# The order of an inverse and a forward transform inside two slots of a hybrid encoder kernel

## The chip, the cores and the metric

The kernel runs on one core of one Trainium2 chip. The metric is the device time of one launch in microseconds. The core has five engines with a queue each: TensorE (PE in the rows, its weight loads PEld), VectorE (DVE), ScalarE (ACT), GpSimd (POOL), and SyncE (SP), which here only starts transfers. They meet at semaphores.

## The reference, cut to what matters

One encoder layer is applied to two sequences, 512 and 256 tokens long, with 1024 features and float32 values. One large projection feeds windowed attention, an order-2 Hyena long convolution and two gates; the branches are merged and projected, and an MLP and a last norm follow. The change concerns the Hyena branch alone. Each of its two rounds convolves 512 channels with a filter as long as the sequence, by a Fourier transform, and multiplies by another row set:

```python
def long_conv(u, spec, bias):
    L = u.shape[1]
    uf = u.astype(jnp.float32)
    y = jnp.fft.irfft(jnp.fft.rfft(uf, n=2 * L, axis=1) * spec[None], n=2 * L, axis=1)[:, :L]
    return y + uf * bias.astype(jnp.float32)
...
    z = x1.astype(jnp.float32) * long_conv(v, spec[:, 0], hyena_bias[0])
    z = x2.astype(jnp.float32) * long_conv(z, spec[:, 1], hyena_bias[1])
```

## The kernel before, in words

All matmuls of the projection keep features on the partitions and the 768 tokens of both sequences along the free axis, in two halves of 384. Float32 precision comes from splitting each operand into a high and a low part and adding three products. Before the merge there are 34 **slots** (`t` from 0 to 33, `T_MERGE` = 34). In each slot TensorE runs `gemm(t)`: one 128-column weight tile against the whole input, 48 matmuls on L739. Behind the gemm it runs the **stages** that the list `STAGES[t]` names. The same list is read by the loops of ScalarE and VectorE, so one list sets the order on three engines: on TensorE and ScalarE as it stands, on VectorE sorted so that an inverse always comes last. Slots 18 to 33 compute the gate columns.

**The Hyena work** is cut into six steps (`STEPS`, numbered 0 to 5 in the code): for each of the two rounds two channel halves of the long sequence, then the whole short sequence. Steps 0, 1, 3 and 4 are the long ones (`LONG`); the "second and fifth step" are numbers 1 and 4. A step goes through this chain:

- `fold(n)`, GpSimd (L655 to L681): sums and differences of each row with its mirror image. A long step takes four instructions (L673, L674, L680, L681), a short one two (L680, L681).
- `turn(n)`, TensorE (L968, matmuls on L981): eight transposes into two PSUM banks. ScalarE copies their high part (L1403), VectorE takes the low part (L2030).
- `forward(n)`, TensorE (L984): for a long step 12 matmuls of 512 columns on L995 into four banks.
- `cosines_out(n)`, ScalarE (L1412), long steps only: copies banks 0 and 2 (L1423).
- `products(n)`, VectorE; for a long step `products_long` (L1967): four rotations (L1977, L1978), which count up `rot_done` after each pair, two multiplications by the filter spectrum over 2048 columns (L1986, L1987), two sums over 1024 columns (L1990, L1991), four `scalar_tensor_tensor` instructions that write the product tile Y (L1997, L1998). The writes of Y first wait for the previous step's inverse, which reads the same tile.
- `inverse(n)`, TensorE (L1010): 32 matmuls of 128 columns on L1029 into two banks, 16 for each.
- `inverse_out(n)`, ScalarE (L1425): copies the two banks (L1431).
- `unfold(n)`, GpSimd (L683): four instructions for a long step (L695, L696, L698, L699), two for a short one (L702, L703).
- `combine(n)`, VectorE (L2040, instruction L2047): the multiplication by the other rows.

GpSimd's own order is written out by hand: `fold(0)`, and then for each n `fold(n + 1)`, `unfold(n)`. So `fold(2)` stands behind `unfold(0)` in its queue, and `fold(5)` behind `unfold(3)`.

**PSUM banks.** The stages share four banks of the tensor `wk` in rotation. A planner (`use`, `bank_of`, `last_reader`, L307 to L339) walks the slots in the order of `STAGES`, gives each use the next bank and has `take` (L928) wait until the last reader of the bank's previous content is done. A long forward's four banks are released by its two cosine copies and its two pairs of rotations in turn.

**Other queues.** SyncE loads the weight tile of slot t + 2 and, in odd slots from 21 on, the two spectrum tiles of the step whose turn stands in slot t (L521), after the previous step's products are done. ScalarE and VectorE split the weight tile of slot t + 2 (L1249, L1691) ahead of their stages of slot t.

The stages of the slots concerned: slot 20 has forward 0, slot 21 turn 1, slot 22 inverse 0 and forward 1, slot 23 turn 2, slot 24 inverse 1 and forward 2, slot 25 turn 3 and inverse 2, slot 26 forward 3, slot 27 turn 4, slot 28 inverse 3 and forward 4, slot 29 turn 5, slot 30 inverse 4 and forward 5, slot 31 inverse 5.

Of the kernel before, what the change touches and what calls it, by code (L numbers as in the profile page):

```python
# [50 lines left out]
T_Q, T_K, T_V, T_HY, T_GATE, T_MERGE, T_OUT, T_MLP = 0, 4, 5, 6, 18, 34, 42, 50  # L51
# [13 lines left out]
LONG = [n for n, (u, _) in enumerate(STEPS) if UNITS[u][0] == 0]  # L65
# [8 lines left out]
STAGES = {t: [] for t in range(T_MERGE)}  # L74
# [3 lines left out]
for _n in range(len(STEPS)):  # L78
    STAGES[T_GATE + 1 + 2 * _n].insert(1 if _n == 0 else 0, ("turn", _n))
    if _n - 1 in LONG:  # L80
        STAGES[T_GATE + 2 + 2 * _n].append(("inverse", _n - 1))
    STAGES[T_GATE + 2 + 2 * _n].append(("forward", _n))
    if _n not in LONG:
        STAGES[T_GATE + 3 + 2 * _n].append(("inverse", _n))

# [2508 lines left out]
```

## Time and profile before

| what | value |
|---|---|
| three runs | 1138.15, 1138.93, 1141.29 us |
| median | 1138.93 us |
| the profiled execution, its time | 1140.42 us |
| its span, first to last instruction | 1138.9 us |
| TensorE busy | 1103.2 us, 97% |
| VectorE busy | 815.6 us, 72% |
| ScalarE busy | 436.4 us, 38% |
| GpSimd busy | 110.7 us, 10% |
| mean granted TensorE clock | 0.993 |

The span is what the engines' records cover; the profiled execution's own time is 1.5 us more. Starts in timelines count from the span's start. A duration in a timeline runs from the instruction's start to its end and includes what it was held up by once it had begun; the time in square brackets is idle time of the engine ahead of it, with what ended it. The granted clock is a share of TensorE's full 2.4 GHz, so that 0.50 is 1.2 GHz.

### The profile page before, as it was taken

Reading aid. Unit: us, or ns where it says so; the run is one execution under the profiler, and the core shown is the slowest. Engines: PE = TensorE matmul, PEld = TensorE weight load, DVE = VectorE, ACT = ScalarE, POOL = GpSimd, SP = SyncE. Lnnn points to the kernel's source line nnn. Section 1 sums busy time; section 2 is a strip of 40 time slices with the busy share of each in tenths; the row PEclk is TensorE's granted clock in tenths of the full one; section 3 lists DMA queues with packets and bytes.
Section 4 is the critical chain, followed back from the end, with each engine's and each line's share of the span. In section 5 each row is a group of like instructions: output and inputs, shape, how many; then the busy total and the mean of one; then the engine's idle time right before and its main releaser. Section 6 shows DMA issues by size and latency. Waiting matters only on the chain. (4 is left out here: it accounts for less than half of the span.)

```text
span 1138.9 us, 16657 instructions
## 1 busy us (share of the span) xinstructions
PE 1103.2 (97%) x6322; PEld 1026.1 (90%) x6322; DVE 815.6 (72%) x1375; ACT 436.4 (38%) x748; POOL 110.7 (10%) x132
## 2 busy tenths in 40 slices
PE   6999999999999999999999999999999999999996
PEld 4777788888899998999889999998999999999886
DVE  5878998778667677456547677687877878688534
ACT  5722145445532222422326332153352625257424
POOL 3101210000314532000000000000000000000000
PEclk9999999999999999999999999999999999999998
DMA  9925572231342332564312342133223323222203
GB/s 351 404 68 171 188 246 87 83 102 40 120 136 102 102 102 102 171 231 140 108 40 111 101 140 74 55 129 107 99 93 111 103 84 116 89 75 74 93 20 111
DMA packets 45525, 138.85 MB, mean 122 GB/s; under 512 B 5051, under 2 KB 10635, under 8 KB 44556
## 3 DMA queue, kind: packets, MB, share of 16 engines
q1 hardware_dynamic: 29024, 80.21, 21.0%
q0 software_dynamic: 11376, 44.84, 11.2%
q10 hardware_dynamic: 5052, 12.81, 3.2%
q8 instruction: 47, 0.77, 0.3%
q14 instruction: 26, 0.21, 0.0%
HBM read 121.61 MB, written 15.74 MB: 121 GB/s over the span
## 5 line engine op out<-in xcount | busy, mean ns | idle before, releaser
L739 PE MATMUL acc_ps<-act_hilo,w_hi 128*128 128x384 f32 x1536 | 339.6, 342 | 2.1 <-DVE w_lo L1691 1.2
L739 PEld LDWEIGHTS acc_ps<-act_hilo,w_hi 128*128 128x128 f32 x1536 | 270.4, 189 | 20.8 <-issue 19.4
L739 PE MATMUL acc_ps<-act_hilo,w_lo 128*128 128x384 f32 x768 | 195.9, 336 | 0.0
L739 PEld LDWEIGHTS acc_ps<-act_hilo,w_lo 128*128 128x128 f32 x768 | 139.5, 189 | 0.0
L1173 PE MATMUL acc_ps<-hidden_hilo,act_hilo 128*128 128x384 f32 x768 | 135.0, 335 | 0.6 <-DVE hidden_hilo L2240 0.4
L1173 PEld LDWEIGHTS acc_ps<-hidden_hilo,act_hilo 128*128 128x128 f32 x768 | 133.1, 188 | 1.9 <-issue 1.0
L1691 DVE TENSOR_TENSOR w_lo<-w_raw,w_hi 128x1024 fp32r<-128x1024 f32 x62 | 76.6, 1236 | 67.7 <-ACT w_hi L1249 66.4
L1249 ACT ACTIVATE w_hi<-w_raw 128x1024 fp32r<-128x1024 f32 x62 | 65.2, 1053 | 40.5 <-PE acc_ps L739 36.9
L2126 DVE SCALAR_TENSOR_TENSOR xT<-acc_ps,modT,xT 128x512 f32<-128x512 f32 (+1 forms) x32 | 19.7, 617 | 61.3 <-PE acc_ps L818 61.1
L2251 DVE SCALAR_TENSOR_TENSOR xT<-acc_ps,modT,xT 128x384 f32<-128x384 f32 (+2 forms) x96 | 40.5, 477 | 31.4 <-PE acc_ps L1173 31.4
L1782 DVE CUSTOM_DVE_ANT_0 dot_out<-dot_ring,c_rows,vecT 128x1024 f32<-128x1024 f32 x48 | 61.6, 1283 | 0.9
L739 PE MATMUL acc_ps<-hidden_hilo,w_hi 128*128 128x384 f32 x256 | 54.7, 334 | 0.0
L1473 ACT ACTIVATE gates_out<-acc_ps 128x768 f32<-128x768 f32 x16 | 13.0, 812 | 102.8 <-PE acc_ps L739 102.8
L818 PE MATMUL acc_ps<-hidden_hilo,w_down_hilo 128*128 128x512 f32 (+1 forms) x288 | 50.2, 336 | 0.0
L818 PEld LDWEIGHTS acc_ps<-hidden_hilo,w_down_hilo 128*128 128x128 f32 x288 | 44.4, 190 | 5.6
L1154 PE MATMUL wk<-act_hilo,w_hi 128*128 128x384 f32 x192 | 48.7, 334 | 0.0
L1154 PE MATMUL wk<-t_hilo,w_hi 128*128 128x384 f32 x192 | 48.7, 334 | 0.0
L2233 DVE TENSOR_TENSOR c_st<-wk,c_st 128x384 f32<-128x384 f32 x84 | 44.7, 550 | 1.7 <-PE wk L1154 1.1
L739 PEld LDWEIGHTS acc_ps<-hidden_hilo,w_hi 128*128 128x128 f32 x256 | 45.3, 188 | 0.0
L2240 DVE TENSOR_TENSOR hidden_hilo<-c_st,hidden_hilo 128x384 fp32r<-128x384 f32 x48 | 26.8, 557 | 23.6 <-ACT hidden_hilo L1585 23.3
L1566 ACT ACTIVATE act_hilo<-w_raw 128x512 fp32r<-128x512 f32 x32 | 20.0, 626 | 59.0 <-PE acc_ps L1173 59.0
L1557 ACT ACTIVATE w_hi<-s_sum 128x512 fp32r<-128x512 f32 x24 | 14.9, 627 | 64.2 <-DVE s_sum L2208 64.2
(284 smaller groups left out, 2017.2 us busy)
## 6 DMA issues: line engine op xcount, KB each, us to landing
w_raw<-in_w_pre SPq DMA_DIRECT2D x50, 512.0 KB, 3.5
dot_ring<-in_w_ada_cols POOLq DMA_DIRECT2D x48, 512.0 KB, 3.9
w_raw<-in_w_up SPq DMA_DIRECT2D x32, 512.0 KB, 3.9
w_raw<-in_w_down SPq DMA_DIRECT2D x16, 512.0 KB, 3.5
w_raw<-in_w_down_half SPq DMA_DIRECT2D x32, 256.0 KB, 2.6
spec<-filt_out POOLq DMA_DIRECT2D x12, 512.0 KB, 3.9
gate_spill<-gates_out ACTq DMA_DIRECT2D x16, 384.0 KB, 2.5
hy_spec<-spec SPq DMA_DIRECT2D x12, 512.0 KB, 5.2
```

The lines of the kernel that those rows point to most:

```text
L739: mm = pe.matmul(acc_ps[:, slot, 512 * h:512 * h + HALF], w[:, kw, :], src[:, x, k, HALF * h:HALF * h + HALF], start=(first and i == 0), s ...
L818: mm = pe.matmul(acc_ps[:, slot, half(h)], w_i[:, k, :], src[:, x, k, half(h)], start=(n == 0 and i == 0), stop=(n == KD - 1 and i == 2))
L1154: mm = pe.matmul(st_ps(q, j), w[:, k, :], st_act(j, x, k), start=(k == 0 and i == 0), stop=(k == PK - 1 and i == 2))
L1173: mm = pe.matmul(acc_ps[:, m % 2, 512 * h:512 * h + HALF], w[:, k, :], hid[:, x, k, HALF * h:HALF * h + HALF], start=(k == 0 and i == 0), ...
L1249: act_e.activation(whi[s][:] if to is None else to[0], raw[s][:], ACT.Copy).then_inc(hi_done, 1)
L1566: act_e.activation(st_weight(ST_DOWN[m % 3])[0], quarter(m % 4), ACT.Copy).then_inc(sd_hi, 1)
L1691: dve.tensor_tensor(lo, raw[s][:], hi, ALU.subtract).then_inc(lo_done, 1)
L1782: dve.tensor_tensor_reduce(junk[:], ring[:, i], cb[:, g], 1.0, vT[:, V_BA + mt:V_BA + mt + 1], ALU.mult, ALU.add, modT[:, mt, g:g + 1]).th ...
L2126: dve.scalar_tensor_tensor(row, acc_ps[:, s, half(h)], modT[:, gate + m, h:h + 1], row, ALU.mult, ALU.add)\
L2233: dve.tensor_tensor(dst, st_ps(q, j), other, ALU.add).then_inc(st_u, 1)
L2240: dve.tensor_tensor(hid_block(q, b, 1), c_block(b), hid_block(q, b, 0), ALU.subtract).then_inc(h4_lo, 1)
L2251: last = dve.scalar_tensor_tensor(xT[:, m, a:b], acc_piece(s, a, b), modT[:, G2 + m, g:g + 1], xT[:, m, a:b], ALU.mult, ALU.add)
```

## The change

In the list of stages, `forward` is no longer appended in even slots. It is inserted at the front for long steps, and at place 1 for short ones:

```diff
     STAGES[T_GATE + 1 + 2 * _n].insert(1 if _n == 0 else 0, ("turn", _n))
     if _n - 1 in LONG:
         STAGES[T_GATE + 2 + 2 * _n].append(("inverse", _n - 1))
-    STAGES[T_GATE + 2 + 2 * _n].append(("forward", _n))
+    STAGES[T_GATE + 2 + 2 * _n].insert(0 if _n in LONG else 1, ("forward", _n))
     if _n not in LONG:
         STAGES[T_GATE + 3 + 2 * _n].append(("inverse", _n))
```

The lists that differ are those of slots 22 and 28: forward 1 ahead of inverse 0, and forward 4 ahead of inverse 3. Slots 20 and 26 hold a forward alone; in slots 24 and 30 a short forward at place 1 stands behind the inverse as it did. No instruction of work is added or removed. Three things follow from the list by program: TensorE's order and ScalarE's order in the two slots, and the banks there. The inverse now takes the places of the forward's first two banks, so its first half waits for the first cosine copy and its second half for the first pair of rotations.

## Rows read from the trace of the kernel before

**Rows 1.** the profile page, part 1: busy time of each engine over the span

```profile
PE 1103.2 (97%) x6322; PEld 1026.1 (90%) x6322; DVE 815.6 (72%) x1375; ACT 436.4 (38%) x748; POOL 110.7 (10%) x132
```

**Rows 2.** the waits of TensorE: waiter <- releaser, total us, times, longest

```profile
PE wk L981 <- POOL hy_fold L681: 4.8, 2, 2.4
```

**Rows 3.** TensorE's timeline, slots 22 to 24: start, us, line, [idle before <-releaser]

```profile
334.18 3.73 PE L1029 MATMUL wk<-dft_inv,hy_prod 128*128 128x128 f32 x32
337.67 0.47 PE L995 MATMUL wk<-hy_foldT_hi,dft_fwd_hi 128*128 128x512 f32 x1
...
340.52 0.87 PE L739 MATMUL acc_ps<-act_hilo,w_hi 128*128 128x384 f32 x4
...
351.41 1.97 PE L981 MATMUL wk<-ident,hy_fold 128*128 128x128 f32 x8 [2.38 <-POOL hy_fold L681]
...
354.83 0.86 PE L739 MATMUL acc_ps<-act_hilo,w_hi 128*128 128x384 f32 x4
```

**Rows 4.** TensorE's timeline of the second stall, in slot 29

```profile
429.46 1.89 PE L981 MATMUL wk<-ident,hy_fold 128*128 128x128 f32 x8 [2.38 <-POOL hy_fold L681]
```

**Rows 5.** TensorE: the clock granted at 352 us (busy, clock, DMA, GB/s)

```profile
352.00:353.00 1.00, 1.00 (x7) 0.50 0.07 16
```

**Rows 6.** TensorE's timeline, slots 25 to 27

```profile
379.90 3.84 PE L1029 MATMUL wk<-dft_inv_p,hy_prod 128*128 128x128 f32 x32 [1.71 <-DVE hy_prod L2023]
...
391.90 0.39 PE L995 MATMUL wk<-hy_foldT_hi,dft_fwd_hi 128*128 128x512 f32 x1
...
403.01 1.04 PE L981 MATMUL wk<-ident,hy_fold 128*128 128x128 f32 x8
...
404.96 0.85 PE L739 MATMUL acc_ps<-act_hilo,w_hi 128*128 128x384 f32 x4
```

**Rows 7.** ScalarE's timeline, slot 22, then slot 26

```profile
337.95 0.60 ACT L1431 ACTIVATE hy_halves<-wk 128x512 f32<-128x512 f32 x1 [1.19 <-PE wk L1029]
...
393.76 1.08 ACT L1423 ACTIVATE hy_cosines<-wk 128x512 f32<-128x512 f32 x2
```

**Rows 8.** GpSimd's timeline, slots 22 and 23

```profile
338.63 1.29 POOL L695 TENSOR_TENSOR hy_pairs<-hy_halves 128x512 f32<-128x512 f32 x1 [29.44 <-ACT hy_halves L1431]
...
341.25 1.29 POOL L698 TENSOR_TENSOR hy_y<-hy_pairs 128x512 f32<-128x512 f32 x1
342.50 3.34 POOL L699 TENSOR_TENSOR hy_y<-hy_pairs 128x512 f32<-128x512 f32 x1
345.81 3.33 POOL L680 TENSOR_TENSOR hy_fold<-hy_xv 128x512 f32<-128x512 f32 x1
349.11 2.25 POOL L681 TENSOR_TENSOR hy_fold<-hy_xv 128x512 f32<-128x512 f32 x1
```

**Rows 9.** VectorE's timeline, slots 22 and 23

```profile
342.27 2.42 DVE L1986 TENSOR_TENSOR hy_cross<-hy_turned,hy_spec 128x2048 f32<-128x2048 f32 x1
344.62 3.38 DVE L1987 TENSOR_TENSOR hy_turned<-hy_turned,hy_spec 128x2048 f32<-128x2048 f32 x1
348.03 2.19 DVE L1990 TENSOR_TENSOR hy_turned<-hy_turned,hy_cross 128x1024 f32<-128x1024 f32 x1
350.15 2.29 DVE L1991 TENSOR_TENSOR hy_turned<-hy_turned,hy_cross 128x1024 f32<-128x1024 f32 x1
```

**Rows 10.** VectorE's timeline, slot 26

```profile
395.77 0.74 DVE L1978 SCALAR_TENSOR_TENSOR hy_turned<-hy_cosines,vecT,wk 128x512 f32<-128x512 f32 x1
...
397.96 2.29 DVE L1986 TENSOR_TENSOR hy_cross<-hy_turned,hy_spec 128x2048 f32<-128x2048 f32 x1
...
402.49 1.23 DVE L1990 TENSOR_TENSOR hy_turned<-hy_turned,hy_cross 128x1024 f32<-128x1024 f32 x1
...
404.88 0.75 DVE L1997 SCALAR_TENSOR_TENSOR hy_prod<-hy_turned,vecT 128x512 f32<-128x512 f32 x1
```

**Rows 11.** the queue that loads the spectra, and the landing times of those loads

```profile
331.16 1.20 SPq L521 DMA_DIRECT2D hy_spec<-spec  x2
...
DMA to landing us min/median/max: 4.3/5.2/7.0
```

## The prediction

> **What bounds the kernel now.** The page's first part comes first: TensorE is busy for 97% of the span [rows 1], so a microsecond counts only where TensorE loses or wins it. The waits of TensorE come next: two of them, 4.8 us together, are the transposes of a turn waiting for the last GpSimd instruction of a fold [rows 2]. The timeline puts the first in slot 23: gemm 23 has run out, TensorE is idle for 2.38 us, and turn 2 starts at 351.41 [rows 3]. The second has the same length in slot 29, ahead of turn 5 at 429.46 [rows 4]. These are exactly the slots behind the two that the change touches.
>
> Each stall has a second price. At 352 us the granted clock is 0.50, the lower level of 1.2 GHz, though TensorE is busy all the while [rows 5]. From the turn's start to the second group of high-part matmuls of the next gemm it takes 354.83 - 351.41 = 3.42 us [rows 3]; the same stretch in slot 27, where nothing was waited for, takes 404.96 - 403.01 = 1.95 us [rows 6]. So a stall now costs 2.38 us plus 1.47 us of slow clock. After the wait of 1.71 us in slot 25 an inverse takes 3.84 us against 3.73 [rows 3, 6], so a wait of that length brings no slow clock.
>
> Why is the fold late? GpSimd's timeline shows a chain of six instructions in its queue: the four of unfold 0, from 338.63, and the two of fold 2, ending at 349.11 + 2.25 = 351.36 [rows 8], 0.05 us before the turn. The first three take about 1.25 us each, the last three 3.34, 3.33 and 2.25. VectorE's timeline beside it reads like a zip: L1986 ends at about 344.62, the fourth GpSimd instruction ends 1.2 us later at 345.84; L1987, which had started at 344.62, takes 3.38 instead of some 2.2, to 348.00; the next GpSimd instruction ends at 349.14, L1990 at 350.22, the last GpSimd one at 351.36, L1991 at 352.44 [rows 8, 9]. Undisturbed, L1986 takes 2.29 and L1990 1.23 [rows 10]. So GpSimd's additions and VectorE's two-input operations on SBUF exclude each other for whole instructions, and take turns. Net durations in this zip are 1.15 us for one of GpSimd, 2.2 for a large and 1.1 for a small one of VectorE.
>
> **The change, part by part.** In slot 22 an inverse and a forward change places on TensorE and ScalarE; slot 28 repeats it with steps 3 and 4. Nothing is added or removed, so TensorE's work costs the same. The inverse takes 337.67 - 334.18 = 3.49 us and the forward 340.52 - 337.67 = 2.85 us [rows 3].
>
> *Forward 1* moves ahead by 3.49 us and starts at 334.18. Slot 26 has a forward with no inverse ahead of it and is the pattern: forward at 391.90 [rows 6], two cosine copies back to back from 393.76 [rows 7], the first pair of rotations done at 395.77 + 0.74 = 396.51, L1986 at 397.96 [rows 10]. Carried over, the first copy starts 1.86 us after the forward, at 336.04, and half of their 1.08 us later it is done, at 336.6; the first rotations are done at 334.18 + 4.61 = 338.79; L1986 starts at 334.18 + 6.06 = 340.24, some 2.2 us before it can really work today. The spectrum that L1986 reads was ordered from 331.16 in two issues, done by 332.36, and such loads land after at most 7.0 us [rows 11]: 339.4 at the latest, so this stays hidden by a margin of 0.9.
>
> *The inverse's new waits.* It starts at 334.18 + 2.85 = 337.03, after the copy that its first bank needs. Its second half starts 1.75 us later, at 338.78, when the rotations that it now waits for are just done. I take 0.1 us. Queued behind it on TensorE is gemm 23, and behind that gemm lies a stall of 2.38 us; up to this length the wait costs nothing, so the sum has 0 for it.
>
> *Unfold 0.* The second half of the inverse is copied at 337.95 now, 3.77 us after the inverse's start, in 0.60 us [rows 7], and GpSimd begins 0.08 us after that. Afterwards: 337.03 + 3.77 + 0.60 + 0.08 = 341.48, which is 2.85 us later. Queued behind it on GpSimd is fold 2, and for fold 2 waits turn 2. **This is what the change costs.**
>
> *The zip.* With both starts known I lay out the turns. L1986 holds from 340.24 to 342.44. GpSimd 1 (waiting since 341.48) to 343.6, L1987 to 345.8, GpSimd 2 to 346.95, L1990 to 348.05, GpSimd 3 to 349.2, L1991 to 350.3, GpSimd 4 to 351.45. Now VectorE comes to the four L1997 and L1998, 0.75 us each with the next starting after about 0.66 [rows 10]. Their two tensors lie in SBUF too, but no row shows such an instruction beside GpSimd. The bounds: they don't exclude GpSimd, or they do like the rest. The nearest rows are those of L1990 and L1991 [rows 9], with two SBUF inputs also, so I take the second: L1997 to 352.1, GpSimd 5 to 353.25, L1998 to 353.9, GpSimd 6 to 355.05. Turn 2 starts at 355.1 instead of 351.41: **3.7 us** later. If they don't exclude it, the last two run in 1.25 us each after 351.45, and the turn starts at 354.0, 2.6 us later.
>
> On this the Trainium skill has a rule (SBUF — State Buffer, section Who interferes with whom): a VectorE instruction with two SBUF inputs contends with a GpSimd instruction that reads SBUF, and the later one fully blocks until the other is done. The trace agrees for the plain additions and multiplications; for `scalar_tensor_tensor` no row shows it, and by the rule the turn would be late by the 3.7, not the 2.6.
>
> *The slow clock.* It is there already. The stall grows from 2.4 to about 6 us, of which no row here has an example in mid-kernel. The nearest row is the present stall, so I add nothing; bounds: it could save its 1.47 us, or cost once more as much.
>
> *Other work.* VectorE's writes of Y (from about 351.5) wait for inverse 0, done by 340.6: free. It ends combine 0 and the weight split for slot 25 near 359, while gemm 24 starts near 356.7 and, like gemm 23 (340.52 to 351.41 - 2.38), takes 8.5 us: hidden. SyncE's next spectrum load is ordered after that, against a need that itself moved by 3.7 us: hidden. Turn 2 takes the banks of the forward's third and fourth use, read long before. In slot 24 both VectorE and GpSimd start from TensorE's work again, so the shift passes on unchanged, with the 1.71 us wait of slot 25 [rows 6].
>
> **Sum.** Two slots by 3.7 is 7.4 us. From the profiled execution: span 1138.9 + 7.4 = 1146.3, and its own time 1140.42 + 7.4 = 1147.8. That execution was 1.5 us above the median of the runs, so against the median: 1138.93 + 7.4 = **1146.3 us**.
>
> **The rivals.**
> - *The four L1997 and L1998 do not exclude GpSimd.* Two slots by 2.6 is 5.2: 1144.1 us. For it speaks only that no row shows the clash. Chance 0.17.
> - *The longer stall is also a longer stretch of slow clock,* 1.47 us more in each: 1149.2 us. Against it: the clock is at its lower level already and had no further to fall. Chance 0.13.
> - *It comes out faster.* One mechanism: at the shared access to SBUF GpSimd wins every time once it has begun. Then its six instructions run from 342.44 in about 7.2 us, turn 2 starts at 349.7, 1.7 us earlier than now, and with a stall of only 0.7 us the slow clock would go too: 2 x (1.7 + 1.47) = 6.3 us, 1132.6 us. It decides when VectorE's large operations come to lie behind the GpSimd chain; what counts is a turn before 351.41. For it speaks that VectorE's operations do start 2.2 us earlier relative to TensorE; against it the strict turns of today's rows. Chance 0.04.
> - *No change to be told.* The no-clash case (5.2) together with a slow clock that by luck is over sooner (up to 2.9 saved) gives 2.3 and 1141.2 us. Chance 0.06.
>
> **How the numbers follow.** My forecast (1146.3) has 0.60, the four rivals 0.40. A measurement of this kernel can tell about 0.3%, 3.4 us, from no change. Slower by more than that: forecast, no-clash and longer slow clock, 0.90. Within: 0.06. Faster: 0.04. The range goes from the no-clash case less 0.8 of the runs' spread, 1143.3, to the longer slow clock plus the same, 1150.0; the faster and the unchanged case stay outside.
>
> **What would show it.** In the profile afterwards: TensorE's wait for L681 at 12 us in two, not 4.8; GpSimd's chain in slot 22 starting about 7.3 us after the slot's first stage with its first instruction already stretched to some 2 us; L1986 starting 2 us earlier relative to the forward's old place. From the first stage of slot 22 to turn 2 it takes 351.41 - 334.18 = 17.2 us now; I forecast 20.9, the no-clash case gives 19.8, and anything under 18.5 refutes both, or if L1998 beside a GpSimd instruction keeps its 0.75 us.

## The result and the profile after

The changed kernel takes 1148.58 us in the median of six runs (1146.21 to 1151.99), against 1139.32 us of the kernel before in the runs beside it: a ratio of 1.0081, 95% interval 1.0058 to 1.0104. It is slower by 9.3 us, with 6.6 to 11.9 us left open by the interval. The forecast was 1146.3 us, 7.4 us over the median of 1138.93 us that it started from.

The page's first part, after, answers to [rows 1]. TensorE's work is 0.7 us more, the span 8.0 us more (1138.9 to 1146.9), so most of what was lost is idle time:

```profile
PE 1103.9 (96%) x6322; PEld 1026.2 (89%) x6322; DVE 821.1 (72%) x1375; ACT 436.4 (38%) x748; POOL 111.8 (10%) x132
```

The waits of TensorE (waiter, releaser, total, times, longest) answer to [rows 2]. The first went from 4.8 to 11.1 us, 6.3 us more; the other, in slots 25 and 31, is what it was:

```profile
PE wk L981 <- POOL hy_fold L681: 11.1, 2, 5.6
...
PE wk L1029 <- DVE hy_prod L2023: 2.1, 2, 1.7
```

TensorE's timeline of slots 22 to 24, and of the second place in slots 28 to 29 (answers to [rows 3, 4]):

```profile
334.64 0.39 PE L995 MATMUL wk<-hy_foldT_hi,dft_fwd_hi 128*128 128x512 f32 x1
...
337.41 3.94 PE L1029 MATMUL wk<-dft_inv,hy_prod 128*128 128x128 f32 x32
341.11 0.94 PE L739 MATMUL acc_ps<-act_hilo,w_hi 128*128 128x384 f32 x4
...
355.26 1.97 PE L981 MATMUL wk<-ident,hy_fold 128*128 128x128 f32 x8 [5.56 <-POOL hy_fold L681]
...
358.69 0.85 PE L739 MATMUL acc_ps<-act_hilo,w_hi 128*128 128x384 f32 x4
...
416.12 0.39 PE L995 MATMUL wk<-hy_foldT_hi,dft_fwd_hi 128*128 128x512 f32 x1
...
436.74 1.97 PE L981 MATMUL wk<-ident,hy_fold 128*128 128x128 f32 x8 [5.56 <-POOL hy_fold L681]
...
440.37 0.86 PE L739 MATMUL acc_ps<-act_hilo,w_hi 128*128 128x384 f32 x4
```

The forward now begins slot 22's stages at 334.64, the inverse follows at 337.41, gemm 23 at 341.11. Turn 2 comes 355.26 - 334.64 = 20.62 us after the first stage; before it was 17.23. The stall ahead of it is 5.56 us, not 2.38. The turn and the start of the next gemm take 358.69 - 355.26 = 3.43 us, as before (3.42). In the second place the figures are 436.74 - 416.12 = 20.62 against 429.46 - 412.24 = 17.22, 5.56 against 2.38, and 440.37 - 436.74 = 3.63 against 433.05 - 429.46 = 3.59. So between the two traces 3.39 + 3.40 = 6.8 us lie in the two stretches from the slot's first stage to the turn: 3.18 us in each stall, and 0.2 us in each inverse ahead of it. Of the other 1.2 us of the spans' difference, 0.46 lies ahead of slot 22, where the kernels are the same, and 0.7 behind slot 29.

GpSimd's timeline, the same six instructions as in [rows 8]:

```profile
342.06 2.08 POOL L695 TENSOR_TENSOR hy_pairs<-hy_halves 128x512 f32<-128x512 f32 x1 [32.41 <-ACT hy_halves L1431]
344.10 3.34 POOL L696 TENSOR_TENSOR hy_pairs<-hy_halves 128x512 f32<-128x512 f32 x1
347.51 2.15 POOL L698 TENSOR_TENSOR hy_y<-hy_pairs 128x512 f32<-128x512 f32 x1
349.62 2.25 POOL L699 TENSOR_TENSOR hy_y<-hy_pairs 128x512 f32<-128x512 f32 x1
351.83 1.71 POOL L680 TENSOR_TENSOR hy_fold<-hy_xv 128x512 f32<-128x512 f32 x1
353.50 1.71 POOL L681 TENSOR_TENSOR hy_fold<-hy_xv 128x512 f32<-128x512 f32 x1
```

And VectorE's beside it, answering to [rows 9, 10]:

```profile
338.51 0.74 DVE L1978 SCALAR_TENSOR_TENSOR hy_turned<-hy_cosines,vecT,wk 128x512 f32<-128x512 f32 x1
...
340.69 2.29 DVE L1986 TENSOR_TENSOR hy_cross<-hy_turned,hy_spec 128x2048 f32<-128x2048 f32 x1
342.90 3.38 DVE L1987 TENSOR_TENSOR hy_turned<-hy_turned,hy_spec 128x2048 f32<-128x2048 f32 x1
346.32 2.19 DVE L1990 TENSOR_TENSOR hy_turned<-hy_turned,hy_cross 128x1024 f32<-128x1024 f32 x1
348.44 2.31 DVE L1991 TENSOR_TENSOR hy_turned<-hy_turned,hy_cross 128x1024 f32<-128x1024 f32 x1
350.78 1.64 DVE L1997 SCALAR_TENSOR_TENSOR hy_prod<-hy_turned,vecT 128x512 f32<-128x512 f32 x1
352.34 1.75 DVE L1998 SCALAR_TENSOR_TENSOR hy_prod<-hy_turned,vecT 128x512 f32<-128x512 f32 x1
354.01 1.74 DVE L1997 SCALAR_TENSOR_TENSOR hy_prod<-hy_turned,vecT 128x512 f32<-128x512 f32 x1
355.68 0.74 DVE L1998 SCALAR_TENSOR_TENSOR hy_prod<-hy_turned,vecT 128x512 f32<-128x512 f32 x1
```

All six of GpSimd's are stretched now, where three were before. Read the two lists as one: L1986 begins at 340.69 with nothing in its way, and the first GpSimd instruction, begun at 342.06, waits it out (2.08 us instead of 1.25). From there the ends alternate: GpSimd 344.14, VectorE 346.28, GpSimd 347.44, VectorE 348.51, and so on. The last four of VectorE are the `scalar_tensor_tensor` of which no row beside GpSimd stood ahead of the prediction: there three of them take 1.64 to 1.75 us, the fourth, alone, 0.74. They exclude GpSimd like the rest.

Measured from the slot's first stage, GpSimd's chain starts 342.06 - 334.64 = 7.42 us in, where it started 338.63 - 334.18 = 4.45 us in before [rows 8], 2.97 us later. From its first start to its last end it takes 355.21 - 342.06 = 13.15 us, where it took 351.36 - 338.63 = 12.73. So of the 3.39 us by which it ends later, 2.97 are the later start and only 0.42 are added stretching.

TensorE's granted clock in the second place (stretch, length, busy, clock, DMA share, GB/s):

```profile
432.00:433.00 1.00, 0.00 (x0) 1.00 0.11 43
...
435.00:436.00 1.00, 0.00 (x0) 0.50 0.00 0
...
438.00:439.00 1.00, 1.00 (x6) 0.50 0.00 0
...
440.00:441.00 1.00, 1.00 (x6) 0.86 0.00 0
```

The clock fell during the idle time, stood at 1.2 GHz for the rest of it and for the first 3.5 us or so of work, then rose. In the first place it fell late: by half-microseconds the granted clock is 1.00 up to 354.5 us, 0.94 up to 355.0, 0.50 from there to 358.0 and 0.65 up to 358.5, so that about 3.1 us of work lie at the low level there.

### The profile page after: what moved, and what is told of

Its sections match the earlier page's. It is cut to its first block and busy times, and to the rows that moved or that the text cites. A ratio compares the mean times of both kernels' runs of the same rounds, so it can differ in the third digit from the quotient of the medians.

```text
span 1146.9 us, 16657 instructions
## 1 busy us (share of the span) xinstructions
PE 1103.9 (96%) x6322; PEld 1026.2 (89%) x6322; DVE 821.1 (72%) x1375; ACT 436.4 (38%) x748; POOL 111.8 (10%) x132
```

## The experiments

All runs are single-core and timed in turns with the kernel before, on one chip for each group of four (the last group has two); ratios are to the kernel before in the same group, whose median lay between 1140.5 and 1141.3 us there (for the change itself it is the ratio of the section above, beside 1139.32 us). A second ruler beside the time is the distance in the trace from slot 22's first stage to turn 2, and from slot 28's to turn 5: it holds nothing of the drift from run to run.

| kernel | ratio, 95% interval | slot 22 to turn 2, us | turn 2 to the gemm's second group, us | slot 28 to turn 5, us |
|---|---|---|---|---|
| before | 1 | 17.23 | 3.42 | 17.22 |
| the change | 1.0081 [1.0058, 1.0104] | 20.62 | 3.43 | 20.62 |
| slot 22 alone | 1.0040 [1.0025, 1.0056] | 20.62 | 3.36 | 17.22 |
| slot 28 alone | 1.0032 [1.0017, 1.0048] | 17.22 | 3.45 | 20.62 |
| the change, fold first | 0.9942 [0.9922, 0.9962] | 14.88 | 1.94 | 14.90 |
| before, fold first | 0.9930 [0.9907, 0.9954] | 14.68 | 1.95 | 14.68 |
| the change, products held | 1.0002 [0.9988, 1.0017] | 15.12 | 1.97 | 15.09 |
| before, products held | 0.9997 [0.9987, 1.0007] | 14.68 | 1.94 | 14.68 |
| the change, stall filled | 1.0046 [1.0030, 1.0063] | 20.64 | 1.98 | 20.65 |
| before, stall filled | 0.9957 [0.9941, 0.9973] | 17.21 | 1.97 | 17.23 |

**One slot at a time.** The condition of the change is `_n == 1` in the one kernel and `_n == 4` in the other:

```diff
-    STAGES[T_GATE + 2 + 2 * _n].insert(0 if _n in LONG else 1, ("forward", _n))
+    STAGES[T_GATE + 2 + 2 * _n].insert(0 if _n == 1 else 1, ("forward", _n))
```

> The order is changed in slot 22 alone; slot 28 stays as before. Theory A (the late inverse holds up the fold in GpSimd's queue, the same in both slots, and each of the two is on the path by itself): half of the loss, about 4 us over before (3.4 us more stall, some tenths of slow clock), with TensorE's wait of 5.6 us in slot 23 and of 2.4 us in slot 29. Theory B (the new wait of the inverse on the rotations carries the loss): also half, but with TensorE's stall in slot 23 unchanged at 2.4 us and the time lost ahead of gemm 23. Theory C (the loss is one of the two alone): 0 or 8 us.

> The order is changed in slot 28 alone. Theory A: about 4 us over before, wait of 2.4 us in slot 23 and 5.6 us in slot 29. Theory C: the complement of the first run.

Measured: 1145.38 us and 1143.99 us, by the ratios 4.6 us (2.9 to 6.4) and 3.6 us (1.9 to 5.5) over the kernel before. TensorE's timeline, slot 22 alone:

```profile
354.13 1.97 PE L981 MATMUL wk<-ident,hy_fold 128*128 128x128 f32 x8 [5.58 <-POOL hy_fold L681]
...
432.10 1.94 PE L981 MATMUL wk<-ident,hy_fold 128*128 128x128 f32 x8 [2.37 <-POOL hy_fold L681]
```

and slot 28 alone:

```profile
351.40 1.73 PE L981 MATMUL wk<-ident,hy_fold 128*128 128x128 f32 x8 [2.37 <-POOL hy_fold L681]
...
433.05 1.97 PE L981 MATMUL wk<-ident,hy_fold 128*128 128x128 f32 x8 [5.58 <-POOL hy_fold L681]
```

The stall is 5.58 us where the order is changed and 2.37 us where it is not. The loss is two equal losses that add up. Theory C falls. Theory B falls too: it wanted the time lost ahead of gemm 23 and the stall left at 2.4 us.

**The fold ahead of the unfold.** GpSimd's order is changed and nothing else. `fold(2)` needs turn 1 and rows that nobody writes, and `fold(5)` needs turn 4 and what the combine of step 2 wrote, so they need not stand behind `unfold(0)` and `unfold(3)`:

```diff
             fold(0)
             for n in range(len(STEPS)):
-                if n + 1 < len(STEPS):
+                if n + 1 < len(STEPS) and n + 1 in LONG:
                     fold(n + 1)
+                if n + 2 < len(STEPS) and n + 2 not in LONG:
+                    fold(n + 2)
                 unfold(n)
```

> The changed kernel with one more edit on GpSimd: fold 2 stands ahead of unfold 0 and fold 5 ahead of unfold 3 in its queue. Theory A: turn 2 and turn 5 no longer wait for anything, so both stalls (2 x 5.6) and their slow clock (2 x 1.5) go: 14 us under the changed kernel, 1134 to 1135 us, under the kernel before too. Theory B: the inverse's wait stays and only the part that stood there before (2 x 3.9) goes: about 1140 us.

> The kernel before with the same edit on GpSimd. Both theories: its two stalls of 2.4 us and their slow clock go, 7.7 us, to about 1131.5 us. Theory A: within 1 us per slot of the run before this one, since the order of the two transforms then has nothing left to hold up; theory B: that run stays 7 to 8 us slower than this one.

Measured: 1134.61 us on the changed kernel, 1131.98 us on the one before. TensorE's timeline of the first (lines stand two lower in these kernels):

```profile
334.08 0.39 PE L997 MATMUL wk<-hy_foldT_hi,dft_fwd_hi 128*128 128x512 f32 x1
...
348.96 1.04 PE L983 MATMUL wk<-ident,hy_fold 128*128 128x128 f32 x8
...
449.12 3.84 PE L1031 MATMUL wk<-dft_inv_p,hy_prod 128*128 128x128 f32 x32 [1.76 <-DVE hy_prod L2025]
```

and of the second:

```profile
332.79 3.73 PE L1031 MATMUL wk<-dft_inv,hy_prod 128*128 128x128 f32 x32
...
347.47 1.04 PE L983 MATMUL wk<-ident,hy_fold 128*128 128x128 f32 x8
...
446.05 3.84 PE L1031 MATMUL wk<-dft_inv_p,hy_prod 128*128 128x128 f32 x32 [0.39 <-DVE hy_prod L2025]
```

Neither turn waits. The change that cost 3.4 us a slot costs 14.88 - 14.68 = 0.2 us a slot once the fold is out of the way. That 0.2 is the inverse's new wait on the rotations: the inverse takes 3.94 us in the trace after, against 3.73 [rows 3], and in its middle, at 339.3 to 339.6 us, there are fewer matmuls than elsewhere in it; the first pair of rotations ends at 338.51 + 0.74 = 339.25. Some 1.4 us more are in slot 31, where inverse 5 waits 1.76 us for VectorE's products instead of 0.39. Those products begin later too, 438.35 us against 435.37 in the other kernel, or 2.4 us after forward 5 against 1.2; why was not tested. In three other places of the same trace VectorE waits for a spectrum load, 3.8 us together, and nowhere in the other kernel's. The two spans differ by 3.5 us; 1.3 of it lies ahead of slot 22. So theory A holds, with a small part of B beside it. The kernel before with the fold first is the fastest kernel of this study, 0.7% under the kernel before (interval 0.5 to 0.9%).

**The clash taken away, the late start left.** In steps 1 and 4 VectorE waits with its large operations until GpSimd is through:

```diff
                 dve.wait_ge(rot_done, m + 2)
+                if n in (1, 4):
+                    dve.wait_ge(fold_done, n + 2)
                 z = Z[:].rearrange("p k (i o) n -> p k i (o n)", o=2)
```

> The changed kernel; in steps 1 and 4 VectorE waits with L1986 until GpSimd has finished the next fold. GpSimd's queue keeps its order and its late start; only the clash with VectorE is taken away. Theory A with the zip as its second half (the inverse's 2.85 us alone would be hidden): GpSimd's six instructions take 7.5 us from 342.1 and end at 349.6, when gemm 23 ends too; the stall is under 0.5 us instead of 5.6, the slow clock goes, and the time is about 14 us under the changed kernel, 1134 to 1136 us. Rival (the start of the unfold is what counts, the clash little): the stall shrinks by less than 2 us a slot. Second rival (VectorE now late, inverse 1 and forward 2 wait for it): the stall moves to slot 24 and little is won.

> The kernel before with the same wait on VectorE. Theory A: GpSimd's chain ends at 346.2, well inside gemm 23; both stalls and their slow clock go, 7.7 us: about 1131.5 us. Second rival: VectorE's products end some 4 us later than before and slot 24 waits for them.

Measured: 1140.90 us and 1139.48 us, where some 1135 and 1131.5 were expected. GpSimd's timeline of the changed kernel so held:

```profile
341.48 1.30 POOL L695 TENSOR_TENSOR hy_pairs<-hy_halves 128x512 f32<-128x512 f32 x1 [32.41 <-ACT hy_halves L1431]
342.74 1.29 POOL L696 TENSOR_TENSOR hy_pairs<-hy_halves 128x512 f32<-128x512 f32 x1
344.11 1.29 POOL L698 TENSOR_TENSOR hy_y<-hy_pairs 128x512 f32<-128x512 f32 x1
345.35 1.28 POOL L699 TENSOR_TENSOR hy_y<-hy_pairs 128x512 f32<-128x512 f32 x1
346.59 1.28 POOL L680 TENSOR_TENSOR hy_fold<-hy_xv 128x512 f32<-128x512 f32 x1
347.83 1.29 POOL L681 TENSOR_TENSOR hy_fold<-hy_xv 128x512 f32<-128x512 f32 x1
```

TensorE's:

```profile
334.06 0.39 PE L995 MATMUL wk<-hy_foldT_hi,dft_fwd_hi 128*128 128x512 f32 x1
...
349.18 1.09 PE L981 MATMUL wk<-ident,hy_fold 128*128 128x128 f32 x8
...
378.83 6.63 PE L1029 MATMUL wk<-dft_inv_p,hy_prod 128*128 128x128 f32 x32 [3.72 <-DVE hy_prod L2025]
```

Six instructions at 1.25 us, none stretched, although the first starts 7.4 us after the slot's first stage, as late as in the changed kernel. Turn 2 comes at 15.12 us, not 20.62. This is the split that was wanted: with the clash taken out of both kernels the late start costs 15.12 - 14.68 = 0.44 us a slot; with it, 20.62 - 17.23 = 3.39. Of the 0.44, 0.2 is the inverse's new wait, which is there with the fold first too (14.88), and some 0.24 is the fold. The clash itself costs 2.55 us of the kernel before (17.23 - 14.68) and 5.50 of the changed one (20.62 - 15.12). This does not mean that it stretches the chain by so much more: the chain takes 7.6 us without the clash, 12.73 with it before and 13.15 after. Without the clash there is slack enough behind the chain to hide nearly all of the later start; in the kernel before the clash has used up that slack already, so the 2.97 us come through whole. But the total was missed, and by the second rival in kind: the stall moved, to slots 25 and 31 rather than 24. VectorE's timeline shows the wait that took its place:

```profile
349.25 2.29 DVE L1988 TENSOR_TENSOR hy_cross<-hy_turned,hy_spec 128x2048 f32<-128x2048 f32 x1 [9.27 <-POOL hy_fold L681]
...
368.11 1.29 DVE L2020 TENSOR_TENSOR hy_cross<-wk,hy_spec 128x512 f32<-128x512 f32 x2 [4.59 <-DMA hy_spec<-spec]
```

and SyncE's, the load it waited for:

```profile
361.65 0.90 SPq L521 DMA_DIRECT2D hy_spec<-spec  x2
```

SyncE orders the spectrum of step 2 when step 1's products are done, and behind a weight load whose buffer VectorE frees after them. Held back, VectorE frees both later: the load is ordered 361.65 - 334.06 = 27.6 us after slot 22's first stage, against 359.15 - 334.64 = 24.5 in the changed kernel and 357.94 - 334.18 = 23.8 before. Products 2 wait 4.59 us for it, inverse 2 waits 3.72 us instead of 1.71 and then runs at the low clock, 6.63 us instead of 3.84. TensorE's granted clock there:

```profile
383.00:384.00 1.00, 1.00 (x7) 0.50 0.93 380
384.00:385.00 1.00, 1.00 (x8) 0.64 1.05 372
```

In slot 31 inverse 5 waits 2.12 us instead of 0.40 and takes 5.46 us instead of 3.84. The kernel before, held, loses its gain at the same two places; its rows of slots 23 and 25:

```profile
349.18 1.04 PE L981 MATMUL wk<-ident,hy_fold 128*128 128x128 f32 x8
...
377.92 5.47 PE L1029 MATMUL wk<-dft_inv_p,hy_prod 128*128 128x128 f32 x32 [3.56 <-DVE hy_prod L2025]
```

In its slot 31 inverse 5 waits 2.11 us and takes 5.47. Turns 2 and 5 and the gemms behind them win about 4.0 us each; the two longer waits and the two slow inverses take back 1.85 + 1.63 + 1.71 + 1.63 = 6.8 of these 8. But its load is ordered at 359.12 - 334.50 = 24.6 us, only 0.9 later than before, and products 2 still wait 4.83 us for it: here it is mostly that TensorE comes to forward 2 four microseconds sooner than before. With the fold first, where TensorE comes as soon, VectorE is less held up, the load is ordered at 354.49 - 332.79 = 21.7 us, and nothing waits for it.

**The price of the slow clock.** Ahead of its wait for fold 2 and fold 5 TensorE runs extra matmuls into the bank that the turn overwrites, so that it is never idle:

```diff
+                if n in (2, 5):
+                    c = take("turn", n, 0)
+                    warm(16, to=wk[:, c:c + 256])
                 pe.wait_ge(fold_done, n + 1)
```

> The changed kernel; ahead of its wait for fold 2 and for fold 5 TensorE runs 16 extra matmuls of 256 columns on the identity, about 5 us, into the bank that the turn then overwrites. The stall is filled and not shortened, so this prices the slow clock alone. If it costs 1.5 us a stall (transposes and six matmul groups at 1.2 GHz): 3 us under the changed kernel. If the longer stall of the changed kernel costs more slow clock than the short one, more than 3 us here and less in the run after this. If the clock does not matter: no change.

> The kernel before with 7 such matmuls (about 2.2 us) ahead of the same two waits. The slow clock goes: 3 us under before, about 1136.3 us.

Measured: 1146.82 us, ratio 1.0059 [1.0042, 1.0076], and 1138.61 us, ratio 0.9987 [0.9973, 1.0001]. Both overran; the rows of the first:

```profile
348.55 7.07 PE L789 MATMUL wk<-ones,ident 128*128 128x256 f32 x32
355.46 1.04 PE L984 MATMUL wk<-ident,hy_fold 128*128 128x128 f32 x8
```

The sixteen ran as 32 instructions and took 355.46 - 348.55 = 6.9 us in a stall of 5.6; by these rows the turn came 1.2 us late, and what the clock gave back was nearly eaten. The seven of the other kernel made its turn 0.5 us late (17.70 against 17.23). The rows told how many would fit, twelve and five:

> As the run with 16 extra matmuls, which took 6.9 us and overran the stall of 5.6 us by 1.2 us; 12 take 5.2 us and fit. By the trace of that run the slow clock costs 1.5 us a stall. Expected: the turn starts where it does in the changed kernel (20.6 us after the slot's first stage), the following 1.9 us instead of 3.4, and 3 us in all under the changed kernel, about 1145.5 us.

> The same on the kernel before with 5 extra matmuls, 2.2 us, which fit its stalls of 2.4 us (7 took 3.0 us and overran). Expected: 3 us under before. Together with the run before this one: if both win 3 us, the longer stall costs no more slow clock than the short one, and the whole difference between the kernels is idle time.

Measured: 1146.63 us and 1136.31 us. TensorE's timeline of the first:

```profile
348.78 5.34 PE L789 MATMUL wk<-ones,ident 128*128 128x256 f32 x24
354.52 1.09 PE L984 MATMUL wk<-ident,hy_fold 128*128 128x128 f32 x8 [0.40 <-POOL hy_fold L681]
```

The turn stands where it stood (20.64 us), and the stretch behind it takes 1.98 us instead of 3.43 after the long stall and 1.97 instead of 3.42 after the short one. The slow clock costs 1.45 us behind either, some 3 us a kernel, and the longer stall costs no more of it. By the times the gains were 4.0 us (1.0081 to 1.0046, two groups of runs, with some 3 us either way) and 4.9 us (interval 3.1 to 6.7), against 3.1 at these places in the traces. For the second kernel the spans differ by 4.3 us: 3.1 between slot 22's first stage and inverse 5, 0.9 ahead of slot 22, where the kernels are the same, and 0.3 behind. So what is above 3.1 us is not shown to be a gain.

## Why the prediction was right

**The place and the chain: right.** That the fold in GpSimd's queue carries the cost, behind the unfold that waits for the inverse, was the main step. Moving the fold alone takes 3.4 us a slot down to 0.2. The rest of the chain came out as laid down: the unfold starts 342.06 - 334.64 = 7.42 us after the first stage (7.30 forecast), L1986 at 6.05 (6.06).

**The zip: right, and a little too dear.** Forecast was a turn 3.7 us later, measured 3.4. The open choice was whether L1997 and L1998 exclude GpSimd. They do, but hold it up a little less than was laid down: the two last GpSimd instructions follow each other at 1.67 us from start to start, where 0.65 + 1.15 = 1.80 was given to each pair. This is also what the Trainium skill says (SBUF — State Buffer, section Who interferes with whom) of instructions with two SBUF inputs, and the trace agrees, at 1.64 to 1.75 us against 0.74. The rival without this clash, 2.6 us a slot, is out.

**The new wait of the inverse: right.** 0.1 us was taken, 0.2 measured, hidden behind the stall as said, and visible as 0.2 us a slot only where the stall is gone. The prediction looked only at the gemm behind the inverse; the unfold waits for the inverse as well and so starts 0.12 us later than forecast. That cost nothing either, because GpSimd's first instruction has to wait until L1986 ends, 0.9 us after it began.

**The slow clock: right to add nothing.** 3.43 and 3.63 us against 3.42 and 3.59, though the stall grew from 2.38 to 5.56. The filled stalls confirm it from the other side. That no row of a stall of 6 us stood behind this term was said, so it was a choice and not a derivation. The argument against the rival, that the clock had no further to fall, would not have ruled it out: the low stretch can lie on more work, as it does in the held kernel (below).

**The sum.** 7.4 us were forecast, 6.8 are in the two places in the trace, 8.0 between the spans and 9.3 between the medians. The two single-slot kernels add up to 8.2 by their ratios. Against its larger set of runs later on, the kernel before has a median of 1140.5 us, not 1138.93, and from there the changed kernel is 8.1 us off; but those are other groups of runs, so this shows how far the ruler moves and measures nothing better. What is above 6.8 has no place in the trace where the kernels differ, and part of it lies ahead of slot 22, where they are the same. Whether any of it belongs to the change stays open. So the forecast is 0.3 us a slot too dear in the places and 1.9 us too cheap in the medians; that 1146.3 and 1148.58 lie so close owes something to chance. The 0.8 us that the range allowed for the runs' spread was small: the three runs of the kernel before spanned 3.1 us.

**The rival of a faster kernel** asked that GpSimd win each time. It does not: they take strict turns.

## What to carry to other kernels

To swap two steps on one engine, look at the queues that are fed by the one that goes later, and at what stands behind it there: the work that is late may be of quite another step. Where two engines exclude each other, a chain of short instructions on the one pays the long instructions of the other in between, so a start that is later by a little can end later by a little more (here 2.97 and 3.39 us), and the slack that would have hidden the late start may be used up already. And before a wait is moved to protect a chain, list what the waiting engine frees for others, and what the engine that now comes sooner will ask for: here it was a load, and waiting for it took back nearly all of the gain.

## What was not expected

- `scalar_tensor_tensor` with two SBUF inputs and GpSimd exclude each other as whole instructions: 1.64, 1.75 and 1.74 us beside it, 0.74 alone. The forecast took this, but no row had shown it.
- In slots 23 and 29 an idle time of 2.4 us was followed by the low clock in each kernel that has it, with about 1.5 us lost; one of 1.7 us in slot 25 was not, and one of 2.1 us in slot 31 was. But the length of the stall doesn't set the price here: a stall of 5.56 us cost about 1.5 us, one of 3.56 us 1.6 (an inverse of 5.47 us instead of 3.84) and one of 3.72 us 2.8 (6.63 us). What goes with the price is how much work lies at the low level: 3.1 and 3.5 us of it behind the stalls of 5.56 us, 3.4 us (378.6 to 382.0 us) behind that of 3.56, and 5.9 us (378.8 to 384.7) behind that of 3.72. In each case about half of that time was lost.
- Five small matmuls on the identity ahead of each of two waits, whose result is overwritten, made the kernel before faster: ratio 0.9957 [0.9941, 0.9973].
